# A fused retention, RWKV and expert block: 32 of 256 tokens take their experts' rows by gather, and the dense part covers 224

## What is computed

```
v1, i1 = top_k(s1, 16);  v2, i2 = top_k(s2, 16)
top, idx = top_k(v1[:, None] + v2[None, :], 16)
experts = e1 * 128 + e2;  gates = softmax(top)
act = gelu(einsum('nhkd,nd->nhk', expert_u[experts], x)) * gates
out = einsum('nhk,nhkd->nd', act, expert_v[experts])
```

## Time and profile before

| | us |
|---|---|
| runs (3) | 2414.02 to 2414.74, median 2414.7 |
| profiled execution, whole | 2414.85 |
| its span, first to last instruction | 2412.7 |
| PE / DVE / ACT / POOL busy | 2382.4 / 1500.4 / 1363.9 / 534.4 |
| HBM read | 423.8 MB, 177 GB/s |

### The profile page before, as it was taken

One profiled execution on the slowest core, in us unless ns is written; L12 is line 12 of the kernel. 1 busy time (PEld: TensorE's weight loads), 2 busy tenths in 40 slices (PEclk: granted clock), 3 DMA queues, 4 the chain that ended last, 5 costly groups with the idle time before them and its releaser, 6 DMA issues.

```text
span 2412.7 us, 43151 instructions
## 1 busy us (share of the span) xinstructions
PE 2382.4 (99%) x13978; PEld 2036.8 (84%) x13978; DVE 1500.4 (62%) x2694; ACT 1363.9 (57%) x2511; POOL 534.4 (22%) x414
## 2 busy tenths in 40 slices
PE   9999999999999999999999999999999999999998
PEld 8888788978888888888888888888888888888886
DVE  5568988476565655767445555555566666666666
ACT  5456544355544545777776666666555555555555
POOL 0000201100000004666666565565100000000000
PEclk9999999999999999999999999999999999999999
DMA  7665553056656565656565555555556555566654
GB/s 217 185 194 147 166 172 125 21 153 196 193 191 213 164 185 192 189 183 184 186 186 166 168 162 158 169 160 158 184 194 195 192 191 192 193 198 221 213 192 165
DMA packets 187075, 429.09 MB, mean 178 GB/s; under 512 B 13173, under 2 KB 81271, under 8 KB 186103
## 3 DMA queue, kind: packets, MB, share of 16 engines
q1 hardware_dynamic: 186999, 428.07, 57.2%
HBM read 423.82 MB, written 4.19 MB: 177 GB/s over the span
## 4 chain that ended last, share of the span: by engine, by line
PE 64%; issue 25%; POOL 6%; DVE 3%; ACT 1%; DMA 0%; POOLq 0%; ACTq 0%; SPq 0%
PE PS L470 20%; PE PS L858 10%; PE PS L860 10%; PE PS L859 10%; PE PS L472 9%; POOL w_lo L1323 5%; PE PS L827 2%; PE PS L513 1%; PE PS L515 1%; PE PS L514 1%; POOL big L1295 1%; PE PS L469 1%; DVE w_lo L1335 1%; DVE inv L1562 0%; PE PS L463 0%
## 5 line engine op out<-in xcount | busy, mean ns | idle before, releaser
L901 ACT ACTIVATE w_hi<-raw 128x512 fp32r<-128x512 f32 x1576 | 953.8, 626 | 566.5 <-PE PS L472 283.2
L470 PE MATMUL PS<-act_both,w_hi 128*128 128x512 f32 x3104 | 1097.2, 399 | 7.1 <-DVE w_lo L1335 6.1
L1335 DVE TENSOR_TENSOR w_lo<-raw,w_hi 128x512 fp32r<-128x512 f32 x1192 | 790.6, 689 | 448.4 <-ACT w_hi L901 445.8
L472 PE MATMUL PS<-act_both,w_lo 128*128 128x256 f32 x2910 | 815.6, 280 | 0.0
L470 PEld LDWEIGHTS PS<-act_both,w_hi 128*128 128x128 f32 x3104 | 577.5, 188 | 135.5 <-DVE w_lo L1335 7.9
L1323 POOL TENSOR_TENSOR w_lo<-raw,w_hi 128x512 fp32r<-128x512 f32 x384 | 496.7, 1312 | 765.6 <-ACT w_hi L901 755.8
L472 PEld LDWEIGHTS PS<-act_both,w_lo 128*128 128x128 f32 x2910 | 550.1, 189 | 4.4 <-issue 0.2
L858 PE MATMUL PS<-w_hi,act_both 128*128 128x512 f32 x1024 | 398.5, 389 | 1.7 <-DVE w_lo L1335 1.7
L859 PE MATMUL PS<-w_lo,act_both 128*128 128x512 f32 x1024 | 398.4, 389 | 0.0
L860 PE MATMUL PS<-w_hi,act_both 128*128 128x512 f32 x1024 | 398.4, 389 | 0.0
L1241 ACT ACTIVATE act_both<-big 128x256 fp32r (+1 forms) x256 | 106.9, 417 | 319.0 <-PE PS L860 317.3
(11 more groups left out here) (238 smaller groups left out, 1494.8 us busy)
## 6 DMA issues: line engine op xcount, KB each, us to landing
raw<-in_peer_u_t SPq DMA_DIRECT2D x256, 512.0 KB, 3.5
raw<-in_peer_v SPq DMA_DIRECT2D x256, 512.0 KB, 4.2
raw<-in_w_in SPq DMA_DIRECT2D x180, 512.0 KB, 3.7
raw<-in_w_out SPq DMA_DIRECT2D x32, 512.0 KB, 4.1
raw<-in_peer_w_q SPq DMA_DIRECT2D x32, 512.0 KB, 4.4
raw<-in_w_ret_branch SPq DMA_DIRECT2D x16, 512.0 KB, 4.3
raw<-in_w_rwkv_branch SPq DMA_DIRECT2D x16, 512.0 KB, 4.7
big<-in_x SPq DMA_DIRECT2D x2, 1024.0 KB, 6.1
```

The costliest lines, as they stand in the source:

```text
L470: last = pe.matmul(PS[:, bank, :], wh, act_both[:, kc, :, :].rearrange("p w n -> p (w n)"), start=start, stop=stop)
L472: last = pe.matmul(PS[:, bank, 0:TOK], wl, act_hi[:, kc, :], start=False, stop=False)
L901: act.activation(w_hi[:, slot % 2, hh * 512:(hh + 1) * 512], raw[:, slot, hh * 512:(hh + 1) * 512], ACT.Copy).then_inc(S["unit_hi"], 1)
L1335: dve.tensor_tensor(w_lo[:, slot % 2, cols], raw[:, slot, cols], w_hi[:, slot % 2, cols].bitcast(f32), ALU.subtract).then_inc(S[done], 1)
```

## The change

The first 32 tokens (`SPARSE`) leave the dense part, which keeps 224 (`DT`), in the matrix `G` of 128 x 224.

- Dense products have 448 and 224 moving columns (`mm_dense`), in both stages: in the value stage the values are stationary (8 tiles of 128 channels per unit, each with a 448- and a 224-column matmul), and the output stands channels x tokens. It is summed, turned by 16 transposes per half, and added. Between the halves (`turn_first`) the first half's rows are added to `x1_dram` in DRAM by a GpSimd DMA.
- Gate turns: 28 in place of 32, from pair 35. DVE's loop of gate turns and its value loop are written out.
- Value low parts: DVE makes k = 0, 2, GpSimd k = 1, 3 (`V_SPLIT`).
- Picks of the first 128 tokens are done by pair 11, those of the others by pair 28, with an exponential after each.
- 32 x 128 = 4096 chosen rows are gathered as 32 tiles of 128 rows (1 MB) of `expert_u` (key stage, used in pairs 16 to 62, two of three) and 32 of `expert_v` (value stage, groups 66 to 117), by indirect DMAs that GpSimd issues two groups ahead, into three landing places. DVE multiplies and sums each key tile with the token's row in two steps of 1024 elements and accumulates each value tile in two such steps (`sparse_step`).
- At group 119 (`ADD_AT`) GpSimd adds the sparse rows to `x1_dram` in four DMAs, waiting for each. SP loads group 120 (`FINAL_AT`) after all of them, then the residual.

```diff
-POOL_SLOTS, DVE_SLOTS = (0, 2, 3), (1,)
+U_SPLIT = {"p_split": (0, 2, 3), "d_split": (1,)}
+V_SPLIT = {"p_split": (1, 3), "d_split": (0, 2)}
+UPAIRS = BLOCKS // 2
...
-EXP_AT, PICKED_AT, GATE_AT = 21, 23, 31
+SPARSE = 32
+DT = TOK - SPARSE
+GATE_TURNS = DT // 8
+FIRST_EXP_AT, EXP_AT, PICKED_AT, GATE_AT = 11, 28, 30, UPAIRS - 1 - GATE_TURNS
...
+PICK_TILES = TOPK * 8 * SPARSE // P
+DOT_AT = [16 + 3 * t // 2 for t in range(PICK_TILES)]
+MAC_AT = [66 + 8 * t // 5 for t in range(17)] + [100 + 5 * t // 4 for t in range(PICK_TILES - 17)]
+USED_AT = DOT_AT + MAC_AT
+LANDS = 3
+IDS_AT, ADD_AT, FINAL_AT = 13, 119, 24
...
+            sp.wait_ge(S["x2T_done"], 4)
+            for q in range(4):
+                sp.dma_start(xw[32 * q:32 * q + 32, :], flat(Z(106, 114))[0:SPARSE, :]).then_inc(S["xw_in"], 16)
+            sp.dma_start(inv_high, a["norm2_w"][0].partition_broadcast(P)).then_inc(S["xw_in"], 16)
...
+                for q in range(4):
+                    cols = slice(32 * q, 32 * q + 32)
+                    sp.dma_start(ids[cols, :], big[0:SPARSE, 104, cols].bitcast(u32)).then_inc(S["ids_in"], 16)
+                    sp.dma_start(sgate[cols, :], big[0:SPARSE, 94, cols]).then_inc(S["ids_in"], 16)
...
-                    run_loop(sp, 0, 10, load_v)
-
-                    sp.wait_ge(S["half_used"], 2 * (V0 + BLOCKS + 24))
+                    run_loop(sp, 0, FINAL_AT, load_v)
+
+                    sp.wait_ge(S["half_used"], 2 * (V0 + BLOCKS + 28))
+                    sp.wait_ge(S["rows_added"], 16 * 6)
...
+            def mm_dense(bank, wh, wl, both, start, stop):
+
+                hi_part = both[:, 0, :]
+                if stop:
+                    pe.matmul(PS[:, bank, 0:DT], wl, hi_part, start=False, stop=False)
+                last = pe.matmul(PS[:, bank, 0:2 * DT].rearrange("p (w n) -> p w n", w=2), wh, both, start=start, stop=stop)
+                if not stop:
+                    last = pe.matmul(PS[:, bank, 0:DT], wl, hi_part, start=False, stop=False)
                 return last
...
+            def v_tile(k, j, start, stop):
+                cols = slice(j * P, (j + 1) * P)
+                return mm_dense(j, w_hi[:, k % 2, cols], w_lo[:, k % 2, cols], act2[:, k % 2], start, stop)
...
                 for hh in range(2):
-                    pe.wait_ge(S["unit_split"], u + hh + 1)
-                    for tt in range(2):
-                        last = v_piece(h, k, hh, tt, start, stop)
+                    pe.wait_ge(*split_done("v", it + h * (BLOCKS // 4), k, hh + 1))
+                    for j in range(4 * hh, 4 * hh + 4):
...
+            def low_parts(stage, it, of, m):
+                for k in of["p_split"]:
                     for hh in range(2):
-                        pool.wait_ge(S["unit_hi"], it * 8 + (2 * (U0 + k) + hh + 1))
+                        pool.wait_ge(S["unit_hi"], 8 * m + (2 * k + hh + 1))
...
+            def gather(t):
+
+                if t == 0:
+                    pool.wait_ge(S["ids_in"], 16 * 8)
+                if t >= LANDS:
+                    pool.wait_ge(S["used"], 2 * (t - LANDS) + 2)
+                if t >= PICK_TILES:
+                    pool.wait_ge(S["used"], 2 * PICK_TILES)
...
+                pool.indirect_dma_start(lands[t % LANDS], None, rows, bass.IndirectOffsetOnAxis(ap=ids[:, j:j + 1], axis=0)).then_inc(S[f"landed{t % LANDS}"], 16)
...
+                for tt in range(2):
+                    pool.dma_start(x1_dram[tt * P:(tt + 1) * P, 0:1024], out_rows[:, tt, :], accum_op=ALU.add).then_inc(S["rows_added"], 16)
+                pool.wait_ge(S["rows_added"], 32)
...
+            def add_sparse():
+                pool.wait_ge(S["used"], 4 * PICK_TILES)
+                for q in range(4):
+                    pool.dma_start(x1_dram[0:SPARSE, :], sparse_out[32 * q:32 * q + 32, :], accum_op=ALU.add).then_inc(S["rows_added"], 16)
+                    pool.wait_ge(S["rows_added"], 16 * (3 + q))
+
+            for g in range(2 * UPAIRS):
+                for t in range(2 * PICK_TILES):
+                    if USED_AT[t] - 2 == g:
+                        gather(t)
+                if g == 96:
+                    for c in (1, 3, 5, 7):
+                        pool.wait_ge(S["odd_read"], c // 2 + 1)
+                        pool.tensor_tensor(out_T[:, c, SPARSE:TOK], odd_tiles[:, c // 2, 0, :], odd_tiles[:, c // 2, 1, :], ALU.add).then_inc(S["out_odd"], 1)
+                low_parts("u" if g < UPAIRS else "v", g % UPAIRS, U_SPLIT if g < UPAIRS else V_SPLIT, U0 // 4 + g)
+                if g == 96:
+                    add_rows(g)
+                if g == ADD_AT:
+                    add_sparse()
...
+            def sparse_step(g, w):
+
+                if g not in USED_AT:
+                    return
+                t = USED_AT.index(g)
+                j, half = t % PICK_TILES, slice(1024 * w, 1024 * w + 1024)
+                if w == 0:
+                    dve.wait_ge(S[f"landed{t % LANDS}"], 16 * (t // LANDS + 1))
+                if t < PICK_TILES:
+                    row = land_u[t % LANDS][:, half]
+                    dve.tensor_tensor_reduce(row, row, xw[:, half], 1.0, 0.0, ALU.mult, ALU.add, dots[:, w, j:j + 1]).then_inc(S["used"], 1)
+                    return
...
+                    dve.scalar_tensor_tensor(sparse_out[:, half], row, dots[:, 1, j:j + 1], sparse_out[:, half], ALU.mult, ALU.add).then_inc(S["used"], 1)
...
                     if par == 0:
-                        for k in DVE_SLOTS:
-                            u_lo(i + GATE_AT, k)
+                        u_lo(i + GATE_AT, 1)
+                    sparse_step(i + GATE_AT, par)
...
+            def v_lo(h, it):
+                g = UPAIRS + h * (BLOCKS // 4) + it
+                for k in range(4):
+                    dve.wait_ge(S["act2_hi"], it * 4 + (h * BLOCKS + k + 1))
+                    dve.tensor_tensor(act2[:, k % 2, 1, :], rowof(4 * it + k), act2[:, k % 2, 0, :].bitcast(f32), ALU.subtract).then_inc(S["act2_split"], 1)
+                    if k in V_SPLIT["d_split"]:
+                        for hh in range(2):
+                            lo(it + (V0 + h * BLOCKS) // 4, k, hh, "d_split")
...
+                    if k % 2:
+                        sparse_step(g, k // 2)
```

More of the change, by code:

```diff
@@ L445, in _ @@
                                          a["final_norm_w"][q * 512:(q + 1) * 512].partition_broadcast(P)).then_inc(S["fw_in"], 16)
-                    with sp.Fori(22, BLOCKS // 4) as it:
+                    for it in range(FINAL_AT + 6, BLOCKS // 4):
                         load_v(it)
@@ new lines, in vm, with turn_rows, turn_first @@
+                    last.then_inc(S["half_used"], 1)
+            def turn_rows(c, bank):
+                for tt in range(2):
+                    last = pe.transpose(PS[:, bank + 2 * (c // 4) + tt, (c % 4) * P:(c % 4 + 1) * P], out_T[:, c, tt * P:(tt + 1) * P], ident)
+                last.then_inc(S["rows_T"], 1)
+            def turn_first():
+                for c in range(8):
+                    if c % 2 == 0:
+                        pe.wait_ge(S["out_even"], c // 2 + 1)
+                    else:
+                        pe.wait_ge(S["out_odd"], c // 2 + 1)
+                    if c in (0, 4):
+                        pe.wait_ge(S["out_even"], 3 + c // 4)
+                        pe.wait_ge(S["odd_read"], 3 + c // 4)
+                    turn_rows(c, 4)
@@ new lines, in last_units, with turn_last @@
+            def last_units():
+                def turn_last(c):
+                    pe.wait_ge(S["out_even"], 4 + max(c + 1, 2 if c < 4 else 4))
+                    turn_rows(c, 0)
+                for c in range(8):
+                    for k in (2, 3):
+                        if c == 0:
+                            pe.wait_ge(S["act2_split"], 2 * BLOCKS - 4 + k + 1)
+                        if c % 4 == 0:
+                            pe.wait_ge(*split_done("v", BLOCKS // 2 - 1, k, c // 4 + 1))
+                        last = v_tile(k, c, False, k == 3)
+                    last.then_inc(S["tile_done"], 1)
+                    if c >= 2:
+                        turn_last(c - 2)
+                turn_last(6)
+                turn_last(7)
@@ L890, in _ @@
                 v_blocks(BLOCKS // 4 - 1, final=True)
+                if h == 0:
+                    turn_first()
         @block.scalar
@@ L1194, in hot_gate @@
                     row = hotA[:, 4 * par + t, :]
-                    last = act.activation(row, row, ACT.Copy, scale=eg[:, 2, ds(i * 8 + (4 * par + t), 1)])
+                    last = act.activation(row, row, ACT.Copy, scale=eg[:, 2, ds(i * 8 + (SPARSE + 4 * par + t), 1)])
                 last.then_inc(S[f"hot{par}"], 1)
@@ L1937, in _ @@
                 at, end = (EARLY + (BLOCKS - EARLY) * m // turns for m in (n, n + 1))
-                last = dve.memset(Z(at, end), 1.0)
+                last = dve.memset(G[:, at:end, :], 1.0)
             link(last)
```

244 lines of the change are left out of this document (151 added, 93 removed).

## The result

| | before | after |
|---|---|---|
| runs of the comparison, median (lowest to highest, 4 each), us | 2414.36 (2413.59 to 2414.74) | 2501.31 (2500.48 to 2502.17) |
| profiled execution, its span, us | 2414.85, 2412.7 | 2500.48, 2498.7 |

The ratio is 1.0361, with a 95% interval of 1.0343 to 1.0379: 3.6% slower. The sign and the mechanism named for it held, and the time lies in the range, but the forecast was +30 us and the measurement is +87.

What follows compares the result with a forecast made beforehand. TensorE was taken as the bound, busy 2382.4 of 2412.7 us. The terms summed as 2414.85 - 71.5 - 51.5 + 26 + 58 + 37 + 32 = 2445 us, with a range of 2362 to 2505.

Steps and rivals of the forecast that it cites:

- (a): Key stage: matmul pairs shrink to 448 and 224 columns, 0.3155 us each, -64.5 us; four gate turns fall away, -7.
- Rival B: Both stages: the short matmul shrinks in full, a pair takes 0.307 us; total 2419 us, chance 0.07.
- (b): Value stage: matmuls become the same pairs, -51.5 us; TensorE waits 0.2 us in each of 128 odd units, +26.
- (c): Value stage: sparse DVE steps and GpSimd's splits exclude each other, 0.9 us for each of 64 steps, +58 us.
- Rival A: Both stages: sparse steps slip into DVE's and GpSimd's idle time; total 2371 us or some 2360, chance 0.28.
- (d): Key stage: sparse steps and gather issues delay GpSimd's splits, 1.7 us in 13 pairs, 0.8 in 19 with gate turns, +37.
- (e): Transfers: 64 gathers of 1 MB cost nothing, hidden by the four raw buffers.
- (f): End of the sparse part: SP loads group 120's values only after GpSimd's four awaited transfers, +18 us; smaller terms besides.
- the +2 for the clock: Group 120: TensorE runs at a lower clock after the stall there, +2 us.
- the middle: Between the stages' halves: TensorE waits for eight sums, copies and 16 transposes, +5 us.
- Rival C: GpSimd is the bound: a gather issue takes 3 us, or descriptors are held up; total 2505 us, chance 0.15.

## Why the forecast was right in sign and short in size

By its own steps:

- **(a), right.** Matmul pairs start 0.31 to 0.32 us apart, 0.3135 in the mean (10.03 / 32), forecast 0.3155. In the changed kernel's key stage:

```profile
1348.88 0.37 PE L524 MATMUL PS<-act_both,w_hi 128*128 128x448 f32 x1
1349.09 0.27 PE L526 MATMUL PS<-act_both,w_lo 128*128 128x224 f32 x1
1349.19 0.37 PE L524 MATMUL PS<-act_both,w_hi 128*128 128x448 f32 x1
...
1349.51 0.37 PE L524 MATMUL PS<-act_both,w_hi 128*128 128x448 f32 x1
```

  The short matmul keeps 0.10 to 0.11 us. Rival B had 0.307 a pair and is out: the measured one lies nearer the forecast, and its 2 ns less are 8 us over both stages.
- **(b), right.** 10.49 us a group is 32 x 0.3135 and 0.46 for two odd units, 0.23 each where 0.2 was taken. With DVE's splits it is 10.03.
- **(c), right.** 12.46 - 10.49 = 1.97 for two steps, 0.98 each where 0.9 was taken: 63 us against 58. One input in place of two takes all of it away, so it is the exclusion. Rival A needed under 0.4.
- **(d), right before the gate turns, wrong in them.** There: 1.8 us against 1.7 in 13 pairs. In the gate turns 14.14 - 11.82 = 2.3 in 19 and 0.4 in 9, together 48 us, where 0.8 x 19 = 15 was taken. That is 33 of the 35 us by which the key stage missed (775.8 against 775.2 - 71.5 + 37 = 740.7). **The step that failed is "DVE's own time there, 54% of a turn ... becomes 9 of 11.9: that fits."** It put DVE's time at nothing, and a share of time says nothing of who waits. With value splits on DVE, one input in place of two takes 0.9 off a turn: that is what the 0.8 stood for, and it was about right. DVE's time is 1.0 more, and 0.3 to 0.5 is left in every turn. The sparse step stands between DVE's splits, stretched by GpSimd's, and the sum; ACT stands in its own order behind that sum, and GpSimd's streak behind ACT. ACT's order alone gives the 48 us back, the part of the second input too: GpSimd then has its high parts earlier, with slack for both. The row that told of it was in the trace before: ACT waiting 1.4 us a turn for DVE. Some 4 of the 48 us are the lower clock after the waits, which the forecast had only at group 120.
- **(e), right.** With steps of 8 elements in the value stage the groups with gathers take 10.49, as the others; in the key stage before the gate turns at most 0.4 us could be theirs (10.54 against a median of 10.15 without). An issue takes GpSimd 0.95 to 1.24 us (1.2 taken), a tile's landing 7.0 at the median.
- **(f), right in size, half wrong in cause.** Groups 119 and 120 cost 31.81 + 12.81 - 2 x 10.49 = 23.6, forecast 20; the +2 for the clock in it measured 2.4. But the forecast laid it on SP's wait; the runs show that GpSimd's own four awaited transfers cost 17.8 without SP's, because it owes TensorE splits meanwhile. The first row addition cost 10.1 and not 3, for the same reason:

```profile
2090.63 1.94 POOL L1446 DMA_DIRECT2D x_scratch<-big  x2
2101.99 2.49 POOL L1426 TENSOR_TENSOR w_lo<-raw,w_hi 128x512 fp32r<-128x512 f32 x2 [9.42 <-DMA x_scratch<-big]
```

  GpSimd is away for 11.4 us, where 6 was taken. Groups 64, 95 and 127 cost 12.7 together, where the middle had 5.

The value stage so gives +5 (c), +7 (row addition), +4 (end) and +8 (the three groups), 24 us; it missed by 22 (780.5 against 697.7 - 51.5 + 26 + 58 + 28 = 758.2), since the pairs were a little shorter than forecast. With the key stage's 35 that is 57. Outside the two stages 2.6 us were added where 4 were forecast, which leaves the 56 between 2445 and the profiled 2500.5.

Rival C gives nearly the measured time (2505), but by luck: its mechanism didn't happen, a gather's issue is 1 us and not 3.

## What to carry to other kernels

Shorter matmuls are worth their columns only as long as no engine that feeds them stands, in its order of work, behind one that is late. Ask not whether an engine's added work fits into its share, but which instruction stands behind it in its queue, and follow that through the in-order queues of the others. A wait in the profile that costs nothing now (ACT for DVE, 1.4 us a turn) is where the next delay will go through. And DVE steps with two SBUF inputs shouldn't run beside GpSimd splits on a chain without slack: the idle GpSimd cost 109 us here by taking over half of DVE's splits, some 27 of them because it owed TensorE splits while it awaited its own transfers.

## What the runs showed of the hardware that was not expected

- The blocked one can be DVE too, and for longer than one instruction. In the changed kernel's gate turns a single DVE split, 0.69 us alone, took 3.16 beside two successive GpSimd splits (2.52 us together), the second of which began while DVE's was waiting:

```profile
1408.95 3.16 DVE L1478 TENSOR_TENSOR w_lo<-raw,w_hi 128x512 fp32r<-128x512 f32 x1 [3.43 <-ACT w_hi L986]
```
```profile
1409.04 2.52 POOL L1426 TENSOR_TENSOR w_lo<-raw,w_hi 128x512 fp32r<-128x512 f32 x2
```

  Although DVE's record starts 0.09 us earlier, it ends 0.55 behind the second GpSimd split. The longest dot product took 3.34 us where 1.21 is its median. The forecast had priced one instruction's wait, 1.1 us.
- An addition to DRAM that GpSimd issues and awaits took 4.1 to 6.1 us from one issue to the next for 256 KB, of which 0.75 to 0.90 are the issue.
